# Hybrid conv / sparse-attention / state-space block: conv chunk first, a table of VectorE fill steps, a second conv tile on GpSimd, an earlier load of one norm row

## What is computed

```python
h = rms_norm(x, norm_mix_g)
ca, cg, q, k, v, iq, ik, iw, z, xbc, dt = split(h @ w_in)
u = ca * sigmoid(cg)                       # group A: 512 channels
u = causal_dwconv(u, w[31 taps])           # 31 multiply-adds over positions
u = silu(layer_norm(u))
att = sparse_attention(...)                # group B: indexer scores, top 128 keys of a query, 8 heads
y = ssd_scan(silu(causal_dwconv4(xbc)), dt, ...)  # group C: 4 chunks of 128 positions
y = rms_norm((y + d_skip * xs) * silu(z), ssm_norm_g)
x = x + concat([u, att, y]) @ w_out
h = rms_norm(x, norm_ffn_g)
x = x + (silu(fg) * fa) @ w_down           # fa, fg = dwconv3(h @ w_up)
```

## Time and profile before

| | |
|---|---|
| median of 3 runs | 763.62 us (762.08 to 764.52) |
| the profiled execution | 763.34 us, span 761.6 us |
| mean granted TensorE clock | 0.993 of full speed |
| TensorE busy | 723.9 us (95%) |
| VectorE busy | 475.6 us (62%) |
| ScalarE busy | 333.9 us (44%) |
| GpSimd busy | 102.9 us (14%) |
| mean DMA rate | 91 GB/s |

### The profile page before, as it was taken

The page is one execution under the profiler, slowest core; times in us unless marked ns, Lnnn a source line. Parts: engine busy times, 40 slices in busy tenths (PEclk is TensorE's granted clock), DMA queues, the critical chain, the costliest instruction groups (busy, mean ns, idle before and its releaser), DMA issues.

```text
span 761.6 us, 9551 instructions
## 1 busy us (share of the span) xinstructions
PE 723.9 (95%) x3474; PEld 581.4 (76%) x3478; DVE 475.6 (62%) x727; ACT 333.9 (44%) x502; POOL 102.9 (14%) x83
## 2 busy tenths in 40 slices
PE   4999988799989989999979999999999999999998
PEld 3667876676666768888869888888888888888886
DVE  4357999967999957666665565656565656211222
ACT  6245463678546664722445434443444344221120
POOL 2000567642000003333130000000000000000000
PEclk9999999999999999999989999999999999999999
DMA  8541312311111143022222442334233322323302
GB/s 263 161 146 59 109 55 59 108 56 56 56 56 55 57 166 111 24 89 56 83 56 56 111 110 75 91 110 110 75 91 110 110 83 82 114 108 110 110 2 110
DMA packets 78048, 69.48 MB, mean 91 GB/s; under 512 B 5815, under 2 KB 64535, under 8 KB 78015
## 3 DMA queue, kind: packets, MB, share of 16 engines
q1 hardware_dynamic: 77871, 68.51, 29.3%
q10 hardware_dynamic: 144, 0.52, 0.2%
HBM read 66.91 MB, written 2.12 MB: 91 GB/s over the span
## 4 chain that ended last, share of the span: by engine, by line
PE 70%; DVE 11%; issue 7%; ACT 6%; POOL 5%; DMA 1%; SPq 0%; DVEq 0%; POOLq 0%; ACTq 0%
PE bank L1458 61%; DVE u_acc L570 3%; POOL stats L729 2%; PE bank L1464 2%; DVE w_lo L580 2%; POOL u_acc L749 2%; PE bank L1478 1%; DVE xbcT L1266 1%; ACT w_hi L824 1%; DMA x_in<-in_x 1%; PE bank L1713 1%; PE bank L1687 1%; DVE prob L1245 1%; PE bank L1661 1%; POOL x2n L795 1%
## 5 line engine op out<-in xcount | busy, mean ns | idle before, releaser
L1458 PE MATMUL bank<-h_hi,w_hi 128*128 128x512 f32 (+1 forms) x496 | 194.5, 392 | 1.0 <-DVE h_lo L1097 1.0
L1458 PE MATMUL bank<-h_hi,w_lo 128*128 128x512 f32 (+1 forms) x496 | 191.6, 386 | 0.0
L1458 PE MATMUL bank<-h_lo,w_hi 128*128 128x512 f32 (+1 forms) x496 | 191.4, 386 | 0.0
L580 DVE TENSOR_TENSOR w_lo<-w_raw,w_hi 128x2048 fp32r<-128x2048 f32 x34 | 80.6, 2369 | 80.7 <-ACT w_hi L824 80.6
L1458 PEld LDWEIGHTS bank<-h_hi,w_hi 128*128 128x128 f32 x496 | 94.6, 191 | 26.6 <-issue 9.0
L1458 PEld LDWEIGHTS bank<-h_hi,w_lo 128*128 128x128 f32 x496 | 94.6, 191 | 18.7
L1458 PEld LDWEIGHTS bank<-h_lo,w_hi 128*128 128x128 f32 x496 | 94.7, 191 | 17.5
L824 ACT ACTIVATE w_hi<-w_raw 128x2048 fp32r<-128x2048 f32 x34 | 64.9, 1910 | 80.3 <-PE bank L1458 80.3
L1419 DVE SCALAR_TENSOR_TENSOR f<-bank,prm,f 128x511 f32<-128x511 f32 x88 | 65.8, 748 | 51.2 <-ACT f L1066 44.9
L1066 ACT ACTIVATE f<-bank,prm 128x512 f32<-128x512 f32 x44 | 33.8, 769 | 95.3 <-PE bank L1458 95.3
L1458 PE MATMUL bank<-w_hi,g_hi 128*128 128x512 f32 x176 | 68.5, 389 | 0.0
(11 more groups left out here) (227 smaller groups left out, 1023.9 us busy)
## 6 DMA issues: line engine op xcount, KB each, us to landing
w_raw<-in_w_up SPq DMA_DIRECT2D x44, 512.0 KB, 4.9
w_raw<-in_w_in SPq DMA_DIRECT2D x34, 512.0 KB, 4.8
w_raw<-in_w_down SPq DMA_DIRECT2D x22, 512.0 KB, 4.1
w_raw<-in_w_out SPq DMA_DIRECT2D x12, 512.0 KB, 4.2
x_in<-in_x SPq DMA_DIRECT2D x4, 512.0 KB, 6.7
tbias<-distance_table SPq DMA_DIRECT2D x1, 2048.0 KB, 8.2
x<-in_x SPq DMA_DIRECT2D x4, 512.0 KB, 6.5
out_x<-y_out SPq DMA_DIRECT2D x8, 256.0 KB, 2.0
```

Of the source, the lines that this page charges most:

```text
L580: eng.tensor_tensor(wlo[:, slot, cols], wraw[:, slot, cols], whi[:, slot, cols].bitcast(F32), ALU.subtract).then_inc(ready, 1)
L1458: ins = pe.matmul(o, a, b, start=first and i == 0 and q == 0, stop=last and i == n - 1 and q == 2)
```

## The change

The chunk order starts with ("conv", 0), then ("iq", 0). Chunk 0's three passes therefore write the gate and value of conv tile 0, its evictions move to slot 3, its glu to slot 5. Chunk "iq" is computed in slots 4 to 7, and the indexer steps move to slots 8 to 11. The evenly spread fill of VectorE is replaced by a table: for each slot a string, in which "1", "2", "3" is the next top-k step of that block (33 each) and "a", "d" the next tap of conv tile 0 or 3 (31 each). Slots of the form 4c-3, which hold "lo", have no entry. Tiles 1 and 2 go to GpSimd, one after the other: additions from slot 15 to 43 and from 43 to 65, ScalarE's products one slot earlier. The two tiles share the two product buffers, so the first two products of tile 2 wait for the last addition of tile 1. `xt` is split over slots 65 and 66. `ln` goes from slots 66, 66, 67, 67 to the end (fill) of slots 67, 67, 68, 68; `lnT` keeps its slots and moves to their end. `gf_row` lies in the place of the first two tiles of xs (`xs_tok`) and is loaded when `seg` of chunk 1 has read them (at slot 77).

```diff
-CHUNKS = [("iq", 0), ("conv", 0), ("conv", 1)]
+CHUNKS = [("conv", 0), ("iq", 0), ("conv", 1)]
...
-TOP_SLOTS = {1: (9, 36), 2: (9, 42), 3: (9, 48)}
-DW_SLOTS = [(15, 44), (14, 50), (42, 63), (46, 65)]
-LN_SLOTS = (66, 66, 67, 67)
+FILL = {6: "aa", 7: "aaa", 8: "aaa", 10: "1121", 11: "1212", 12: "31213", 14: "2131", 
+        15: "21321", 16: "32112", 18: "31", 19: "23", 20: "121", 22: "312a3", 23: "1213", 
+        24: "2a13121", 25: "3", 26: "a2", 27: "13", 28: "21a", 30: "2311", 31: "23a12", 
+        32: "3121a3", 33: "123", 34: "12a", 35: "1321", 36: "32a2", 37: "3", 38: "a232", 
+        39: "3a232", 40: "3a23", 42: "2a323", 43: "a3a33", 44: "a33a", 46: "ddd", 47: "a", 
+        48: "ddadd", 50: "da", 51: "dd", 52: "dadd", 54: "dad", 55: "d", 56: "addda", 58: "ddd", 
+        59: "dd", 60: "dddd", 62: "ddd"}
+POOL_SLOTS = {1: (15, 43), 2: (43, 65)}
+LN_SLOTS = (67, 67, 68, 68)
...
-DW_POOL = 0
+DW_POOL = (1, 2)
...
-    put(3, ("ev", "iq", 0), ("ev", "iq", 1), ("small",), ("ev", "ik", 0))
+    put(3, ("ev", "cg", 0), ("ev", "ca", 0), ("small",), ("ev", "ik", 0))
     put(4, ("iwT",), ("dt", 0))
-    put(6, ("dt", 1))
-    put(8, ("dt", 2))
-    for n, b in ((5, 1), (6, 2), (8, 3)):
-        put(n, *[("idx", b, h) for h in range(NIH)])
...
+    put(5, ("dt", 1))
+    put(6, ("ev", "iq", 0), ("dt", 2))
+    put(8, ("ev", "iq", 1))
+    for n, b, hs in ((8, 1, (0, 1, 2, 3)), (9, 2, (0, 1, 2, 3)), (10, 3, (0, 1)), (11, 3, (2, 3))):
+        put(n, *[("idx", b, h) for h in hs])
...
+    for j, (a, b) in POOL_SLOTS.items():
         spread([("dw", j, i) for i in range(CONV_K)], a, b)
...
+        spread([("dwp", j, i) for i in range(1, CONV_K)], a - 1, b - 1)
+    for n, letters in FILL.items():
+        fill[n] += [next(streams[v]) for v in letters]
     for t in range(NT):
-        put(LN_SLOTS[t], ("ln", t))
+        fill[LN_SLOTS[t]].append(("ln", t))
...
-        put(LNT_SLOTS[j], ("lnT", j))
+        fill[LNT_SLOTS[j]].append(("lnT", j))
...
-    put(s0 + 1, *[("xt", t) for t in range(NT)])
+    for t in range(NT):
+        put(s0 + 1 + t // 2, ("xt", t))
...
-        gf_row = at("gf_row", [P, DM], F32, r5)
+        gf_row = at("gf_row", [P, DM], F32, r1 + 8 * K)
...
-                elif s == ("ssdT", NT - 1):
-
-                    evacuated(sp, "yT", NT - 1)
+                elif s == ("seg", 2):
+
+                    sp.wait_ge(xd_ready, 3 * 2)
                     sp.dma_start(gf_row[:, :], norm_ffn_g.to_broadcast([P, DM])).then_inc(s_gf, 16)
...
                     if i > 2:
                         act.wait_ge(dw_taps[j], i - 1)
-                    elif i == 1:
-                        act.wait_ge(glu_ready, j + 1)
+                    else:
+                        if i == 1:
+                            act.wait_ge(glu_ready, j + 1)
+                        if j != DW_POOL[0]:
+
+                            act.wait_ge(dw_taps[DW_POOL[DW_POOL.index(j) - 1]], CONV_K)
...
-                        ins = pe.matmul(ps("iq", v)[:, :], w[:, kk, v], h[:, kk, :],
+                        ins = pe.matmul(ps("cg" if v == 0 else "ca", 0)[:, :], w[:, kk, v], h[:, kk, :],
```

More of the change, by code:

```diff
@@ L124, in make_plan @@
         fill[4 * c - 3].append(("lo", c))
+    streams = {str(b): iter([(k, b, r) for r in range(TOPK // 8) for k in ("topmax", "topmark")]
+                            + [("sel", b)]) for b in (1, 2, 3)}
+    for j in range(4):
+        streams["abcd"[j]] = iter([("dw", j, i) for i in range(CONV_K)])
     def spread(steps, a, b):
@@ L135, in make_plan @@
     put(2, ("prm",))
-    put(3, ("ev", "iq", 0), ("ev", "iq", 1), ("small",), ("ev", "ik", 0))
+    put(3, ("ev", "cg", 0), ("ev", "ca", 0), ("small",), ("ev", "ik", 0))
     put(4, ("iwT",), ("dt", 0))
-    put(6, ("dt", 1))
-    put(8, ("dt", 2))
-    for n, b in ((5, 1), (6, 2), (8, 3)):
-        put(n, *[("idx", b, h) for h in range(NIH)])
-    for b in (1, 2, 3):
-        spread([(k, b, r) for r in range(TOPK // 8) for k in ("topmax", "topmark")], *TOP_SLOTS[b])
-        fill[TOP_SLOTS[b][1]].append(("sel", b))
+    put(5, ("dt", 1))
[3 more added lines that the diff above has]
+        put(n, *[("idx", b, h) for h in hs])
     put(1, ("gtab",))
@@ L175, in make_plan @@
         n = at[("conv", j)]
[L176 to L179, removed]
+        if j:
+            put(n + 2, ("ev", "cg", j))
+            put(n + 4, ("ev", "ca", j))
+        fill[n + 5].append(("glu", j))
+    for j, (a, b) in POOL_SLOTS.items():
         spread([("dw", j, i) for i in range(CONV_K)], a, b)
-        if j == DW_POOL:
-            spread([("dwp", j, i) for i in range(1, CONV_K)], a - 1, b - 1)
+        spread([("dwp", j, i) for i in range(1, CONV_K)], a - 1, b - 1)
+    for n, letters in FILL.items():
+        fill[n] += [next(streams[v]) for v in letters]
     for t in range(NT):
-        put(LN_SLOTS[t], ("ln", t))
+        fill[LN_SLOTS[t]].append(("ln", t))
         front[LN_SLOTS[t] + 1].append(("lnn", t))
     for j in range(4):
-        put(LNT_SLOTS[j], ("lnT", j))
+        fill[LNT_SLOTS[j]].append(("lnT", j))
     for m in range(8):
@@ L740, in _ @@
                     inverse_root(rqk[:, NH * i:NH * i + NH], ssqk[:, NH * i:NH * i + NH], rqk_ready)
-                elif k == "dw" and s[1] == DW_POOL:
+                elif k == "dw" and s[1] in DW_POOL:
                     _, j, i = s
@@ L747, in _ @@
                         pool.wait_ge(dw_taps[j], i)
-                        pool.wait_ge(dwp_ready, i)
+                        pool.wait_ge(dwp_ready, DW_POOL.index(j) * (CONV_K - 1) + i)
                         pool.tensor_tensor(u_acc[:, j, i:], tapped[i % 2][:, 0:SEQ - i],
@@ L762, in _ @@
                         pool.wait_ge(ecs_ready, 1)
-                        pool.wait_ge(dw_taps[DW_POOL], CONV_K)
+                        for j in DW_POOL:
+                            pool.wait_ge(dw_taps[j], CONV_K)
                     else:
@@ L997, in _ @@
                     if t == 0:
-                        act.wait_ge(dw_taps[DW_POOL], CONV_K)
+                        for j in DW_POOL:
+                            act.wait_ge(dw_taps[j], CONV_K)
                     act.activation(dump[:, :], yb[:, :], ACT.Square,
@@ L1170, in _ @@
                         .then_inc(glu_ready, 1)
-                elif k == "dw" and s[1] != DW_POOL:
+                elif k == "dw" and s[1] not in DW_POOL:
                     tap(dve, *s[1:])
@@ L1552, in _ @@
                             pe.wait_ge(hi_evac, HIGH.index(("hT", NT - 1, 1)) + 1)
+                            claim(pe, "cg", 0)
+                            claim(pe, "ca", 0)
                             first_pass(whi, hhi, True, False)
```

## The result

The changed kernel took 772.7 us (median of 4, 770.98 to 775.08) against 764.07 for the one before (4 runs beside it, 762.08 to 765.17). The ratio is 1.0122, 95% interval 1.0089 to 1.0155: slower by 1.2%, where 749.6 and faster was forecast. The profiled execution took 771.46 us, span 769.4, so the span grew by 7.8.

The account below looks back on a forecast made before the run. TensorE was taken as the bound, with some 20 us of idle time and 5 of clock to win back, mostly beside a full VectorE. Gains of -17.3 and losses of +3.6 took 763.3 to 749.6 us, range 744 to 759.

Parts of the forecast that it names:

- Slots 6 to 35: 38 to 150 us: VectorE relieved of taps, -7.5 us of TensorE's idle time, and -1.6 for the first clock fall.
- Rival 2: VectorE or ScalarE stays the bound, and the clock falls as before: 758.7 us; chance 0.21.
- Rival 3: Slots 46 to 65: GpSimd's additions hold VectorE up, 767.9 us at 1.27 us per addition; chance 0.08.
- Slots 36 to 45: 150 to 190 us: ScalarE's extra products and wait for tile 1's last addition in slot 42 cost +2.0 us.
- Slots 46 to 65: 190 to 281 us: fewer VectorE taps outweigh the cost of 26 additions on GpSimd, -3.8 us.
- The split `xt`: Slots 65 and 66: later transposes of the last two xs tiles cover the 2.44 us bank wait, -2.0 us.
- Slots 67 to 70: `ln` of tiles 2 and 3 one slot nearer to `yd` makes TensorE wait, +1.6 us.
- The end: Last norm: `gf_row` asked for at slot 77 instead of 86, so GpSimd's products lie under TensorE's, -2.4 us.
- The second fall of the clock: Half clock near 394.3 us for 6.7 us, costing 3.3 us; the forecast left it in.
- rival 1: The second fall of the clock goes too, 3.3 us less: 746.3 us; chance 0.17.

Follow-up runs that it names:

- e1: Changed kernel with GpSimd's additions of tile 1 over slots 15 to 44 instead of 43, tile 2 over 44 to 65; 753.22 us.
- e9: Changed kernel with ScalarE's products one slot later, in the same slots as the additions, whose ranges stay; 754.23 us.
- e4: Kernel before the change with its one GpSimd tile's additions ending at slot 43 instead of 44, products at 42 instead of 43; 786.41 us.
- e8: e1 with conv tile 2's 31 taps back on VectorE, spread over slots 43 to 63; 758.78 us.
- e12: Kernel before the change with only the xs transposes (`xt`) of the third and fourth tile one slot later; 766.33 us.
- e5: e1 with `lnT` alone put back ahead of the state products of its slot, `ln` left late; 749.62 us.
- e7: Kernel before the change with only `gf_row` at its new place and loaded at slot 77; 760.15 us.
- e10: Changed kernel with tile 1's additions to slot 44, tile 2's to 62, `ln` at the end of slots 66 and 67, `lnT` ahead of state products; 750.45 us.

## Why the prediction was wrong

**Slots 6 to 35, -7.5 and -1.6 forecast, +8.6 came by slot 38.** This is the step that failed, in its sentence "The additions on GpSimd in these slots are 23 instead of 22, the same cost." Their number was right and said nothing. What decides is where each stands against the product that waits for it, and the change from 30 slots to 29 took that from one slot to none for 15 taps. e1, e9 (mended in two ways) and e4 (brought into the kernel before) show it: at slot 38 the distance is worth 8.6 + 8.4 = 17.0 us, 11.4 of them idle time of TensorE. The rest of the step holds in the main. With the distance mended slot 38 starts 8.4 earlier than before, against 9.1 forecast. The reading of VectorE was right, too: in slots 20 to 37 it is busy 55.51 of 62.00 in e1, where it had 65.89 of 69.30. But "lo" came late once still, by 2.25 us, with a half clock behind it, where the forecast had none.

None of the rivals was this. Rival 2 came nearest by its sign (ScalarE's wait for additions), but it took an engine for full, and none was. Rival 3 gave 767.9, nearer to the result than the forecast, but its place was slots 46 to 65, and there the changed kernel won 3.3 us; e8, with fewer additions, is slower there.

**Slots 36 to 45, +2.0; +1.5 came from slot 38 to 46.** Its place is right: in the slots after 42 ScalarE's timeline has the wait for tile 1's last addition,

```profile
190.53 0.69 ACT L1034 ACTIVATE square_dump<-u_in,prm 128x482 f32<-128x482 f32 x1
...
192.50 0.72 ACT L1034 ACTIVATE xskip<-u_in,prm 128x511 f32<-128x511 f32 x1 [1.28 <-POOL u_acc L761]
```

1.28 us against the 1.05 to 1.27 forecast. Behind it ScalarE empties the transposed probabilities at 193.73, and TensorE, which needs them, waits 1.98 us until 194.36, the wait of about 2 us that was forecast behind slot 42. The difference to before grows by 1.6 there. The price is not fixed, though: e1 has the same wait of ScalarE, 1.27 us at 179.39, and loses nothing there (-8.4 at slot 38, -8.8 at slot 46).

**Slots 46 to 65, -3.8; -3.3 came**, in e1 -1.8. VectorE's tap took 0.855 us as a mean, not 0.92, so the additions cost it 0.155 x 38 = 5.9 us on its taps, less than the 8.4 forecast. By the Trainium skill (SBUF — State Buffer, section "SBUF: two separate sides") the shared port is held for a whole instruction and the other engine waits it out. GpSimd's additions, from 1.04 to 4.14 us long, fit that, and so do the 11 taps that met a GpSimd instruction, 1.24 us against 0.73. The 33 us of a full price on VectorE are not there, since only 11 of 39 taps met one.

**The split `xt`, -2.0; -3.5 came at slot 66.** 0.9 of it is two tiles' transposes that only moved past the point. Its sign hung on the later `ln`, which the forecast had not seen (e12).

**Slots 67 to 70, +1.6; +9.1 came from slot 66 to 73.** The wait for `sct` came as forecast, 1.58. Mis-sized is all that was left out: 2.42 for the bank behind `lnT`, which the text of the prediction did not follow to the end of its slot, 3.4 for the two half clocks behind these waits, and 0.9 of transposes moved. These make 8.3; 0.8 I can't place. e5 shows that `lnT`'s move was the dearer part: without it e5 loses 2.8 where e1 loses 7.4.

**The end, -2.4; -1.9 at slot 91**, and 2.35 as a change by itself (e7). The second fall of the clock did not come in the changed kernel (rival 1), 2.7 more. It is there at 382.4 in e5 and 384.2 in e10, which have the early load as well.

The sum: -1.0 to slot 20, then +9.6, +1.5, -3.3, -3.5, +9.1, -1.9 and -2.7 make +7.7 (from unrounded times) of the span's +7.8. That e5's 749.62 is the forecast figure is in part luck: its parts, in the same order to the end of slot 90, are -8.3 (up to slot 38), -0.5, -1.8, -3.5, +2.8 and -2.0, where -9.1, +2.0, -3.8, -2.0, +1.6 and -2.4 were forecast.

## What to carry to other kernels

Where in-order engines hand work to each other through two buffers, count for each step how far, in slots, it stands behind the step it waits for, and look at what stands ahead of that one on its engine. A range made one slot shorter took this from 1 to 0, and the amount of work on each engine stayed the same. It costs where the work ahead hangs, through other engines, on the step that waits, as GpSimd's root does here; tile 2 had distance 0 for most taps and lost nothing by it. The sign in a profile is a stretch in which no engine is full and the same few lines name each other in the waits. A wait that is won early (the bank for xs) may have been the cover of the next one: ask which instruction comes to the front then, and whether its inputs are there.

## What the runs showed that I had not expected

One slot of spacing was worth 22.7 us in e4, of 763.75: a ring of 7.7 us per slot where TensorE has 2.7 of work, and some 9 of the 22.7 are slower products and not waiting. In the changed kernel five waits of TensorE of 1.6 to 3.1 us had 3.4 us at half of the clock behind them, 1.7 us more each, and others as long had none. A fall also left or came in where the edit was far away: e7 touches nothing before slot 77, and its first falls are at 135.1 and 152.1, where before has one, at 151.8. GpSimd's root of 128x8 took 1.65 to 2.11 us in e1, 1.65 to 2.68 before and 2.02 to 4.22 in e4, for the same shape, and in the ring it is counted once per slot.
